# Latent attention with values as the stationary operand for two heads at a time, row sums taken with the exponential, and shares multiplied in before the turn

## Reference

```python
def causal_block_attention(q, k, v, scale):
    ...
        s = jnp.einsum('bhqd,bkhd->bhqk', q_blk, k).astype(jnp.float32) * scale
        q_pos = blk * CHUNK + jnp.arange(CHUNK)
        s = jnp.where(k_pos[None, :] <= q_pos[:, None], s, -jnp.inf)
        p = jax.nn.softmax(s, axis=-1).astype(v.dtype)
        return jnp.einsum('bhqk,bkhd->bqhd', p, v)
```

## Time and profile before

| | |
|---|---|
| time, median of 3 runs | 3390.84 us (3390.18 to 3391.23) |
| profiled execution, its own time | 3390.26 us |
| its span, first to last instruction | 3388.5 us |
| granted TensorE clock, mean | 1.000 |
| TensorE busy / VectorE / ScalarE / GpSimd | 3373.1 / 1648.9 / 1051.0 / 1547.8 us |
| attention loop, layer 0 | 2376.00 to 2412.06 us after the span's start |
| attention loop, layer 1 | 2948.70 to 2984.77 us |

### The profile page before, as it was taken

The page is one execution under the profiler, slowest core; times in us unless marked ns, Lnnn a source line. Parts: engine busy times, 40 slices in busy tenths (PEclk is TensorE's granted clock), DMA queues, the critical chain, the costliest instruction groups (busy, mean ns, idle before and its releaser), DMA issues.

```text
span 3388.5 us, 43407 instructions
## 1 busy us (share of the span) xinstructions
PE 3373.1 (100%) x15434; PEld 2734.7 (81%) x15434; DVE 1648.9 (49%) x2000; ACT 1051.0 (31%) x1412; POOL 1547.8 (46%) x1160
## 2 busy tenths in 40 slices
PE   9999999999999999999999999999999999999999
PEld 7888877788888888887778888887888888788887
DVE  5442236754423644223575442379581727857161
ACT  3222234332222322223443222236421123642122
POOL 4444443354544544444335444453354543435443
PEclk9999999999999999999999999999999999999999
DMA  4332422233332333243223333242232333223332
GB/s 151 99 98 94 112 75 69 75 100 99 93 105 88 102 97 95 98 113 81 63 81 91 98 97 105 84 107 61 63 100 95 98 98 77 61 72 108 94 99 81
DMA packets 496159, 311.26 MB, mean 92 GB/s; under 512 B 41793, under 2 KB 454828, under 8 KB 496044
## 3 DMA queue, kind: packets, MB, share of 16 engines
q1 hardware_dynamic: 494316, 307.21, 31.2%
q10 hardware_dynamic: 1727, 2.45, 0.2%
HBM read 305.94 MB, written 3.67 MB: 91 GB/s over the span
## 4 chain that ended last, share of the span: by engine, by line
issue 38%; PE 32%; POOL 26%; DVE 2%; POOLq 1%; DVEq 0%; DMA 0%; ACT 0%; ACTq 0%
POOL wl L502 26%; PE bank L527 5%; PE bank L531 5%; PE bank L532 5%; PE bank L546 5%; PE bank L550 4%; PE bank L552 4%; PE bank L1154 1%; PE mb L1181 1%; PE mb L609 1%; PE bank L553 1%; DVE sd_p L2305 0%; PE mb L1101 0%; POOLq L499 0%; POOLq L497 0%
## 5 line engine op out<-in xcount | busy, mean ns | idle before, releaser
L502 POOL TENSOR_TENSOR wl<-raw,wh 128x512 fp32r<-128x512 f32 x1152 | 1546.7, 1364 | 1806.6 <-ACT wh L1333 1806.1
L1333 ACT ACTIVATE wh<-raw 128x1024 fp32r<-128x1024 f32 x576 | 608.6, 1057 | 1626.1 <-PE bank L527 825.8
L546 PE MATMUL bank<-xh,wh 128*128 128x512 f32 x2384 | 933.1, 391 | 0.0
L550 PE MATMUL bank<-xl,wh 128*128 128x512 f32 x2384 | 927.7, 389 | 0.0
L552 PE MATMUL bank<-xh,wl 128*128 128x512 f32 x2086 | 811.9, 389 | 0.0
L546 PEld LDWEIGHTS bank<-xh,wh 128*128 128x128 f32 x2384 | 447.4, 188 | 105.0 <-issue 11.8
L550 PEld LDWEIGHTS bank<-xl,wh 128*128 128x128 f32 x2384 | 447.6, 188 | 92.7 <-issue 0.5
L527 PE MATMUL bank<-hh,wh 128*128 128x512 f32 (+1 forms) x1216 | 472.5, 389 | 0.0
L531 PE MATMUL bank<-hl,wh 128*128 128x512 f32 (+1 forms) x1216 | 472.2, 388 | 0.0
L532 PE MATMUL bank<-hh,wl 128*128 128x512 f32 (+1 forms) x1216 | 472.2, 388 | 0.0
L552 PEld LDWEIGHTS bank<-xh,wl 128*128 128x128 f32 x2086 | 391.5, 188 | 81.4
(11 more groups left out here) (420 smaller groups left out, 3166.2 us busy)
## 6 DMA issues: line engine op xcount, KB each, us to landing
raw<-in_ffn_wi_dram SPq DMA_DIRECT2D x176, 512.0 KB, 3.7
raw<-in_mlp_w_dram SPq DMA_DIRECT2D x128, 512.0 KB, 3.8
raw<-in_w_in_dram SPq DMA_DIRECT2D x102, 512.0 KB, 3.7
raw<-in_ffn_wo_dram SPq DMA_DIRECT2D x88, 512.0 KB, 3.6
raw<-in_w_out_dram SPq DMA_DIRECT2D x32, 512.0 KB, 3.8
raw<-in_w_ple_gate_dram SPq DMA_DIRECT2D x16, 512.0 KB, 3.9
raw<-in_w_a_dram SPq DMA_DIRECT2D x8, 512.0 KB, 3.4
raw<-in_w_b_dram SPq DMA_DIRECT2D x8, 512.0 KB, 3.4
```

What stands on the lines that cost most here:

```text
L502: last = gp.tensor_tensor(wl[j][:, part], raw[j % RAW_SLOTS][:, part], wh[j][:, part].bitcast(F32), ALU.subtract)
L546: first = pe.matmul(out[0:width, :], h[:, c:c + width], rh[:, k, :], start=k == 0, stop=False)
L550: pe.matmul(out[0:width, :], h[:, c:c + width], rl[:, k, :], start=False, stop=False)
L1333: act.activation(wh[n % SPLIT_SLOTS][:], raw[n % RAW_SLOTS][:], ACT.Copy).then_inc(s.hi_ready, 1)
```

## The change

The causal mask is no longer a product but an addition by VectorE on the diagonal columns in PSUM, ahead of the reduction. ScalarE's exponential also gives the row sum (`accum_out`). VectorE takes its reciprocal, GpSimd multiplies the block in place by it, and the turn waits for that. The turned probabilities of three heads are kept (`prob_t[0..2]`), and once for two heads TensorE multiplies with the values stationary: two heads in the two column halves of the array, up to 512 columns moving. `head_scaled`, `o_tok` and `pair_turned` are gone. Scores are made four blocks ahead in place of three. Some smaller edits make partial-row operands whole (the gate sums, `pick`, `sel4`, the column of `var`) and move `query(L, 3)` ahead of a wait.

```diff
+LOOK = 4
...
-        prob_t = at_kb("prob_t", 52, [P, 4, S])
+        prob_t = [at_kb(f"prob_t{h}", kb, [P, NT, S]) for h, kb in enumerate((24, 52, 44))]
+        row_sum = small[:, 4:28]
...
+            def shares(L):
+                out = Block2.base_slab + L * B2_SLABS + S2_OUT
+                for c in range(NT * MLA_H):
+                    gp.wait_ge(s.as_ready, at(L, 24, c + 1))
+                    block = prob[:, c % 4, 0:(c % NT + 1) * P]
+                    gp.tensor_scalar(block, block, row_sum[:, c:c + 1], None, ALU.mult).then_inc(s.an_ready, 1)
+                    if c in (5, 9, 13):
+                        gp.wait_ge(s.hi_ready, out + c // 4)
+                        low_part(c // 4 - 1)
+                gp.wait_ge(s.hi_ready, out + 4)
+                low_part(3)
...
-                pe.matmul(B4[0:32 + ML_H, :], const[:, C_GATES:C_GATES + 32 + ML_H], var[:], start=True, stop=True)\
+                pe.matmul(B4, const[:, C_GATES:C_GATES + P], var[:], start=True, stop=True)\
...
-                    last = pe.matmul(B4[:, t:t + 1], var[64:65, t * P:(t + 1) * P], ones[64:65, 0:1], start=True, stop=True)
+                    last = pe.matmul(B4[:, t:t + 1], var[:, t * P:(t + 1) * P], ident[:, 64:65], start=True, stop=True)
...
                     pe.matmul(out[:, 0:(n + 1) * P], q_all[h][:, n * P:(n + 1) * P], k_all[:, h, 0:(n + 1) * P],
-                              start=True, stop=False)
-                    pe.matmul(out[:, n * P:(n + 1) * P], mask16[:, 0, :], mask16[:, 1, :], start=False, stop=True)\
-                      .then_inc(s.al_ready, 1)
+                              start=True, stop=True).then_inc(s.al_ready, 1)
...
-                    pe.wait_ge(s.ae_ready, at(L, 24, c + 1))
+                    pe.wait_ge(s.an_ready, at(L, 24, c + 1))
...
+                def weighted(i):
+                    pe.wait_ge(s.at_copied, at(L, 24, 8 * i + 8))
+                    if i == 1:
                         pe.wait_ge(s.y_read, at(L, 1, 1))
+                    elif i == 2:
+                        pe.wait_ge(s.ao_done, at(L, 3, 1))
+                    for j in range(NT):
+                        for side in range(2):
+                            h = 2 * i + side
+                            last = pe.matmul(mb[64 * side:64 * side + 64, 2 + i % 2, j * P:S], v_tok[:, j, h, 0:64],
+                                             prob_t[h % 3][:, j:NT, j * P:(j + 1) * P], start=j == 0, stop=j == NT - 1)
                     last.then_inc(s.ot_ready, 1)
...
+                for c in range(LOOK):
                     logits(c)
                 for c in range(blocks):
+                    if c + LOOK < blocks:
+                        logits(c + LOOK)
                     turned(c)
+                    if c in (9, 17):
+                        weighted(c // 8 - 1)
+                weighted(2)
...
-                                   bias=small[:, 32 + n:33 + n], scale=-1.0).then_inc(s.ae_ready, 1)
-                    if c:
-                        copied(c - 1)
+                                   bias=small[:, 32 + n:33 + n], scale=-1.0, accum_out=row_sum[:, c:c + 1]).then_inc(s.ae_ready, 1)
+                    if c >= 2:
+                        copied(c - 2)
...
                 query(L, 2)
                 rotary_sums(L)
+                query(L, 3)
                 dve.wait_ge(s.y_squared, at(L, 1, 1))
...
                     dve.wait_ge(s.al_ready, at(L, 24, c + 1))
+                    diagonal = bank[(MLA_BANK + c) % TILE_BANKS][:, n * P:(n + 1) * P]
+                    dve.scalar_tensor_tensor(out=diagonal, in0=mask_qs, scalar=-1.0, in1=diagonal, op0=ALU.mult, op1=ALU.add)
+                    dve.drain()
...
+                def share(c):
+                    dve.wait_ge(s.ae_ready, at(L, 24, c + 1))
+                    dve.reciprocal(row_sum[:, c:c + 1], row_sum[:, c:c + 1]).then_inc(s.as_ready, 1)
...
                 for c in range(blocks):
-                    if c + 2 < blocks:
-                        biggest(c + 2)
+                    if c + LOOK - 1 < blocks:
+                        biggest(c + LOOK - 1)
+                    share(c)
```

More of the change, by code:

```diff
@@ L168, in program @@
         gate_raw = place("gate_raw", [P, KT, 8])
-        sel4 = place("sel4", [ML_H, P])
-        mask16 = place("mask16", [P, 2, P], BF16, offset=union)
+        sel4 = place("sel4", [P, P])
         a_col = place("a_col", [P, NT, SSD_H], offset=union + 1024)
@@ L495, in _, with low_part, low_parts @@
             gp.tensor_copy(rel_wide[:], rel[:, :, None].to_broadcast([33, SW_H, TOEP_REP])).then_inc(s.consts_ready, 1)
[L496 to L504, removed]
+            def low_part(j):
+                for half in range(2):
+                    part = slice(half * (SLAB // 2), (half + 1) * (SLAB // 2))
+                    last = gp.tensor_tensor(wl[j][:, part], raw[j % RAW_SLOTS][:, part], wh[j][:, part].bitcast(F32),
+                                            ALU.subtract)
+                    last.then_inc(s.split_done if half else s.half_split, 1)
+            def low_parts(first, end):
+                with gp.Fori(first // SPLIT_SLOTS, end // SPLIT_SLOTS) as n:
+                    for j in range(SPLIT_SLOTS):
+                        gp.wait_ge(s.hi_ready, n * SPLIT_SLOTS + j + 1)
+                        low_part(j)
+            def shares(L):
[9 more added lines that the diff above has]
+                low_part(3)
+            done = 0
+            for L in range(2):
+                out = Block2.base_slab + L * B2_SLABS + S2_OUT
+                assert out % SPLIT_SLOTS == 0
+                low_parts(done, out)
+                shares(L)
+                done = out + SPLIT_SLOTS
+            low_parts(done, 2 * (B1_SLABS + B2_SLABS))
         @block.tensor
@@ L733, in minus_m @@
                         for side in range(2):
-                            pe.matmul(mb[:, side, :], picked(2 * pair + side), rows_hl[64:96 + SSD_H, :], start=True, stop=True)\
+                            h = 2 * pair + side
+                            pe.matmul(mb[:, side, :], pick[:, h:h + 1].to_broadcast([P, P]), rows_hl[:], start=True, stop=True)\
                               .then_inc(s.bc_ready, 1)
                     else:
-                        pe.matmul(B4, sel4[:], var[0:ML_H, :], start=True, stop=True).then_inc(s.bc_ready, 1)
+                        pe.matmul(B4, sel4[:], var[:], start=True, stop=True).then_inc(s.bc_ready, 1)
                 def scores(pair, j):
@@ L1190, in pair_turned @@
                     last.then_inc(s.ot_ready, 1)
                 blocks = NT * MLA_H
-                for c in range(3):
+                for c in range(LOOK):
                     logits(c)
                 for c in range(blocks):
-                    if c + 3 < blocks:
-                        logits(c + 3)
+                    if c + LOOK < blocks:
+                        logits(c + LOOK)
                     turned(c)
-                    if c:
-                        weighted(c - 1)
-                    if c in (11, 19):
-                        pair_turned(c // 8 - 1)
@@ L1203, in mla @@
-                weighted(blocks - 1)
+                    if c in (9, 17):
+                        weighted(c // 8 - 1)
+                weighted(2)
                 pe.wait_ge(s.ae_ready, at(L, 24, 24))
@@ L2363, in mla @@
                 last.then_inc(s.y_done, 1)
-                for h in range(3, MLA_H):
+                for h in range(4, MLA_H):
                     query(L, h)
@@ L2392, in scan_split @@
                        .then_inc(s.ssd_done, 1)
[L2394 to L2401, removed]
+                def share(c):
+                    dve.wait_ge(s.ae_ready, at(L, 24, c + 1))
+                    dve.reciprocal(row_sum[:, c:c + 1], row_sum[:, c:c + 1]).then_inc(s.as_ready, 1)
                 def pair_split(i):
                     dve.wait_ge(s.ot_ready, at(L, 3, i + 1))
-                    split(xh[:, 5 + i, :], xl[:, 5 + i, :], mb[:, 3, :]).then_inc(s.ao_done, 1)
+                    split(xh[:, 5 + i, :], xl[:, 5 + i, :], mb[:, 2 + i % 2, :]).then_inc(s.ao_done, 1)
                 blocks = NT * MLA_H
-                biggest(0)
-                biggest(1)
+                for c in range(LOOK - 1):
+                    biggest(c)
                 for c in range(blocks):
-                    if c + 2 < blocks:
-                        biggest(c + 2)
+                    if c + LOOK - 1 < blocks:
+                        biggest(c + LOOK - 1)
+                    share(c)
                     if c == 0:
@@ L2520, in constants @@
         pack[2 + half::32, C_BACKK + 64 * half:C_BACKK + 64 * half + 64] = 1.0
-    sel4 = (np.arange(ML_H)[:, None] == r[None, :] // 32).astype(np.float32)
+    sel4 = (r[:, None] == r[None, :] // 32).astype(np.float32)
     pack[:, C_MQS:C_MQS + P] = np.where(r[None, :] <= r[:, None], 0.0, NEG)
```

22 lines of the change are left out of this document (8 added, 14 removed).

## The result

The changed kernel takes 3438.94 us in the median of 4 runs against 3390.51 before: 1.0144 times as long, 95% interval 1.0132 to 1.0156, 48.4 us more. The forecast was 3416, in a range of 3402 to 3438: the right direction, about half the size, and the measured time is 0.9 us above the range.

What follows compares the result with a forecast made beforehand. TensorE bounds the old kernel; the ring would bound the new loop, 50.3 us against 36.06. 14.2 longer less 0.8 and 0.55 is 12.9 a layer, 25.8 in two: 3390.26 becomes 3416 us, range 3402 to 3438.

Steps and rivals of the forecast that it cites:

- the ring: Attention loops: a closed chain of waits over two blocks, 5.76 us a head for even blocks, 5.65 for odd.
- T: TensorE's turn of a block's probabilities in the attention loops, waiting for M: 0.44 us for n = 3, 0.11 a block.
- B: VectorE's step on a block's scores in the loops: mask addition 0.28 us, drain 0.10, reduction 0.28 to 0.69.
- L(c+3): TensorE's score product for the block three after block c, ending 0.44 us (n = 0) to 1.08 (n = 3) after its start.
- I take the copy: Price of GpSimd's multiplication in the loops, taken from its one-input copy: 0.10 us plus 0.18 for each 128 columns.
- M: GpSimd's in-place multiplication of a block by its reciprocal row sum, between reciprocal and T: 0.28, 0.46, 0.65, 0.83 us.
- the low part: GpSimd's low part of a slab in the loop, 2.50 us with 0.97 free: 1.6 over, counted once.
- VectorE's side work: VectorE's other work in the loop beyond its free time: four reciprocals 2.2 us, two splits 1.4, two pair splits 2.0.
- rival 2: GpSimd dearer than any row: another 0.3 us for each M, 4.7 more a layer, 3426 us; chance 0.15 for 3424 to 3440.
- rival 4: TensorE's clock falls to 1.2 GHz in the loops and its steps double: 17 us a layer, 3450 us; chance 0.06.
- the edges: Small edits around the loop: moved query gains 0.8 us a layer, whole-row operands cost nothing.
- Rivals 1 and 3: 1: TensorE stays the bound, faster, 3371 us, chance 0.06. 3: two heads' products don't overlap, 3428 us, chance 0.03.

Runs made afterwards that it cites:

- the kernel with the clock held: The changed kernel with eight idle 128-column transposes a block added on TensorE where it waits for GpSimd: 3426.8 us.

## Why the prediction was wrong in size

**The bound, and the ring: right.** TensorE's own work in the loop fell, to about 29.5 us in the kernel with the clock held (49.6 less 20 of idle transposes, an estimate), where the forecast had 27.9 (36.0 - 5.6 - 1.4 - 1.1); and the loop became longer because its steps follow one another. The order of reciprocal and reduction alone is worth 3.6 to 4.1 us a loop as the kernel stands, and 2.7 with the clock held. Mask addition 0.29, drain and gap 0.07 to 0.10, reciprocal 0.15, products of 2.3: all as priced. One sentence of it was too strong, "nothing of T's went back into B": before, L(c+3) stood behind T(c-1), and T(c+3) behind L(c+3), B(c+3) and E(c+3), so there was a ring then too, over four blocks. The change cut its length in blocks to two and put two more steps in.

**The first step that failed: "I take the copy".** M's term was mis-sized, 0.28 to 0.83 us taken, 0.64 to 1.57 measured, above even the upper bound. Put into the prediction's own sum: the two rings' heads are 6.7 and 6.85 us instead of 5.76 and 5.65, and five heads 34.25 instead of 28.5, 5.75 us more; the start 0.4; M(1) to M(3) at the end 1.8; the low part 0.2; while VectorE's side work, with 0.28 us more room in each of eight blocks, costs 2.2 less. 50.3 + 5.95 = 56.25, and the kernel with the clock held at full shows 56.95, part of which is its idle transposes. That the upper bound could be passed was rival 2, at 0.15. The measured time lies in that rival's range, 3424 to 3440, but not by M alone: with the clock held it is 3426.8. The Trainium skill's rule beside it ("GPSIMD Engine Reference", Performance versus the Vector engine: one input at best 1.8 cycles an element, two inputs 2.6) puts the two forms in the wrong order here: at that page's 1.2 GHz, 0.31 us for each 128 columns is 2.9 cycles an element for the operation with a scalar, and the product with a broadcast column, 0.20 us, is 1.9. The measurement decides.

**The second: the clock, rival 4, held apart as a case of its own.** It was given 0.06 and a price for a fall throughout, 17 us a loop. It fell in parts of the loop, and cost at least 6.5 and 6.0 us. It was not independent of M: the granted clock in the loops is 0.80 and 0.76 with M, 0.93 and 0.89 without, and in layer 0 the clock went down after the loader had stood 3.21 us behind a low part and M(6). But a dearer M is not all of it. In layer 1 it fell with no wait over 2.1 us in the loop before it, about the length that the prediction itself had written down, and it fell without M too; so the forecast should have had some of this in its main case. The Trainium skill's warning ("TensorE: Matmul & The Clock Gate", Why this matters for your kernels) against idle gaps between bursts of matmuls is borne out by this trace, which no row of before could show.

**Third, the edges: mis-sized the other way.** The query was worth its 1.6 us in two layers. The whole-row operands, "I cost them at nothing", gained 3.9. The timelines show it at the gate sums and at the first `pick` product, each time first the kernel before, then the changed one:

```profile
446.76 1.05 PE L707 MATMUL mb<-var,const 128*36 128x512 f32 x2
447.74 0.50 PE L546 MATMUL bank<-xh,wh 128*128 128x512 f32 x1
448.07 0.39 PE L550 MATMUL bank<-xl,wh 128*128 128x512 f32 x1
```
```profile
446.46 1.02 PE L731 MATMUL mb<-var,const 128*128 128x512 f32 x2
446.92 0.79 PE L570 MATMUL bank<-xh,wh 128*128 128x512 f32 x1
447.56 0.40 PE L574 MATMUL bank<-xl,wh 128*128 128x512 f32 x1
```
```profile
471.14 0.39 PE L553 MATMUL bank<-xh,wl 128*128 128x512 f32 x1
471.46 0.72 PE L734 MATMUL mb<-rows_hl,pick 38*128 38x512 f32 x2
...
472.45 0.40 PE L550 MATMUL bank<-xl,wh 128*128 128x512 f32 x1
```
```profile
470.59 0.39 PE L577 MATMUL bank<-xh,wl 128*128 128x512 f32 x1
470.82 0.63 PE L759 MATMUL mb<-rows_hl,pick 128*128 128x512 f32 x2
...
471.52 0.39 PE L574 MATMUL bank<-xl,wh 128*128 128x512 f32 x1
```

With 36 stationary columns the second product behind starts 1.31 us on (446.76 to 448.07), with 128 it starts 1.10 us on, for the same moving columns: 0.21 us. The next start alone, 0.98 against 0.46 us, would say too much, since the product behind then stands longer itself (447.56 - 446.92 = 0.64 us against 0.33). Around the `pick` product, with 38 rows against 128, it is 1.31 us against 0.93 from the product ahead to the second one behind (471.14 to 472.45, 470.59 to 471.52): 0.38 us. The Trainium skill ("TensorEngine Tiling (Array Packing)", Key Properties) says that going from one tiling mode to another drains TensorE. The gaps are what that would give, but no run shows that these products are in a tiling mode of their own. The prediction went by the moving columns, which are the same; the durations of the gate sums' rows hardly differ either (592 to 620 ns against 592 to 595). It shows only in the starts around them.

**The account.** Forecast 25.8; the loops at full clock 13.3 more (2 x 6.65, M and what its sum leaves over); the clock 12.5; the edges 5.5 instead of 1.6, so -3.9: 47.7, against 48.7 from span to span. The missing 1 us lies outside the loops, where 6.6 us were to be gained by this count and 5.6 were. It was not taken apart, and it is no more than the spread there: in the twelve kernels that have the edges the first loop starts between 2370.8 and 2372.1.

**Rivals 1 and 3** fell. No kernel with the new loop came near TensorE's own work as its length, and the two heads do overlap, 2.31 us for two.

## What to carry to other kernels

When a step is put between two steps of an engine that is full, draw the loop that it closes through every engine's fixed order before adding up busy times: here each engine had room, and the loop became 75% longer. Where a price is unknown and multiplies a step of such a ring, its range decides, so bound it by more than the nearest rows; and once TensorE waits, the price of its clock belongs in the main case and not beside it. Read what a matmul costs from the starts of the products on both sides of it, over more than one, and not from its duration.

## What the runs showed of the hardware

- GpSimd: multiplication by a scalar, in place, 0.57 us for 128 columns and 1.49 for 512 with a constant, 0.64 and 1.57 with a scalar for each partition; the same as a product of two tensors with a broadcast column, 0.44 and 1.04.
- TensorE's clock, in the kernel with the multiplication on VectorE: at 1.00 with 8 or with 2 idle transposes of 128 columns before each of 23 turns (with 2 the loop is 44.8 us, TensorE busy 36.6), at 0.89 and 0.93 without them. In the changed kernel, work that computes nothing made it faster by 12.2 us (3438.9 to 3426.8, a single run).
- A product with 36 stationary columns between products with 128 held TensorE 0.21 us longer than one padded to 128, and one with 38 rows 0.38 us longer than one with 128.
